# Feed-forward of a two-block transformer kernel: one 512-column operand against the high weights, 256 columns against the low weights

## What is computed

```python
x = x + 0.5 * swiglu(rms_norm(x, gain), w_gate, w_up, w_down)

def rms_norm(x, g):
    y = x * lax.rsqrt(jnp.mean(x * x, axis=-1, keepdims=True) + 1e-6)
    return y * g

def swiglu(x, w_gate, w_up, w_down):
    return (jax.nn.silu(x @ w_gate) * (x @ w_up)) @ w_down
```

## Time and profile before

| what | value |
|---|---|
| time, median of 3 runs | 1128.37 us (1127.51 to 1128.53) |
| profiled execution | 1127.42 us, of which the span is 1125.6 us |
| granted TensorE clock over the span | 0.994 of 2.4 GHz |
| TensorE busy (matmul) | 1109.3 us, 99%, 8842 matmuls |
| VectorE, ScalarE, GpSimd busy | 62%, 51%, 13% |
| DMA | 200.2 MB, 178 GB/s on average |

### The profile page before, as it was taken

How to read it: one execution, slowest core, us unless ns; L and a number is a source line. 1 busy time by engine, 2 the same in 40 slices (tenths; PEclk the granted TensorE clock), 3 DMA queues, 4 the chain that set the end, 5 groups by cost and what they waited for, 6 DMA issues and landing times.

```text
span 1125.6 us, 22927 instructions
## 1 busy us (share of the span) xinstructions
PE 1109.3 (99%) x8842; PEld 1086.3 (97%) x8842; DVE 697.3 (62%) x953; ACT 571.3 (51%) x826; POOL 145.9 (13%) x181
## 2 busy tenths in 40 slices
PE   8999999998999999999999999999999999999997
PEld 7999999887999999999999999999999999999997
DVE  6655655687786555557565555677856667666543
ACT  6544444564664444445444444544655555444541
POOL 3311100025031111011111100000200012111100
PEclk9999999998999999999999999999999999999998
DMA  8755555553356555556556555545565546555551
GB/s 283 262 185 178 178 188 187 168 165 99 95 174 200 185 176 180 187 169 190 186 185 186 177 182 166 188 168 187 183 189 175 183 148 208 187 185 186 178 179 38
DMA packets 55581, 200.20 MB, mean 178 GB/s; under 512 B 6304, under 2 KB 6304, under 8 KB 55392
## 3 DMA queue, kind: packets, MB, share of 16 engines
q1 hardware_dynamic: 54576, 196.11, 54.1%
q0 software_dynamic: 512, 2.65, 0.6%
q10 hardware_dynamic: 432, 0.57, 0.2%
HBM read 198.26 MB, written 1.05 MB: 177 GB/s over the span
## 4 chain that ended last, share of the span: by engine, by line
PE 93%; DVE 3%; POOL 1%; ACT 1%; DMA 1%; issue 0%; ACTq 0%; DVEq 0%; POOLq 0%
PE pair L1131 30%; PE pair L1132 30%; PE pair L1133 30%; DVE x_hl L744 1%; DVE w_lo L738 1%; PE pair L1345 1%; DMA x<-x_in 1%; POOL x_sq L378 1%; POOL x_sq L370 1%; PE pair L1355 0%; DVE x L755 0%; PE pair L1411 0%; PE pair L1454 0%; POOL qk_a L361 0%; PE pair L1366 0%
## 5 line engine op out<-in xcount | busy, mean ns | idle before, releaser
L738 DVE TENSOR_TENSOR w_lo<-w_raw,w_hi 128x1024 fp32r<-128x1024 f32 x369 | 457.3, 1246 | 347.8 <-ACT w_hi L425 346.6
L1131 PE MATMUL pair<-x_hl,w_hi 128*128 128x256 f32 x1792 | 508.8, 284 | 2.6 <-DVE x_hl L744 1.7
L1132 PE MATMUL pair<-x_hl,w_hi 128*128 128x256 f32 x1792 | 507.1, 283 | 0.0
L1133 PE MATMUL pair<-x_hl,w_lo 128*128 128x256 f32 x1792 | 507.0, 283 | 0.0
L425 ACT ACTIVATE w_hi<-w_raw 128x1024 fp32r<-128x1024 f32 x369 | 386.4, 1054 | 234.1 <-PE pair L1133 221.2
L1131 PEld LDWEIGHTS pair<-x_hl,w_hi 128*128 128x128 f32 x1792 | 343.9, 192 | 4.2 <-issue 2.3
L1132 PEld LDWEIGHTS pair<-x_hl,w_hi 128*128 128x128 f32 x1792 | 343.9, 192 | 0.1
L1133 PEld LDWEIGHTS pair<-x_hl,w_lo 128*128 128x128 f32 x1792 | 343.9, 192 | 0.0
L1131 PE MATMUL pair<-wide,w_hi 128*128 128x256 f32 x960 | 273.3, 285 | 0.7 <-DVE wide L932 0.7
L1132 PE MATMUL pair<-wide,w_hi 128*128 128x256 f32 x960 | 272.3, 284 | 0.0
L1133 PE MATMUL pair<-wide,w_lo 128*128 128x256 f32 x960 | 272.2, 284 | 0.0
(11 more groups left out here) (164 smaller groups left out, 558.4 us busy)
## 6 DMA issues: line engine op xcount, KB each, us to landing
w_raw<-stream SPq DMA_DIRECT2D x369, 512.0 KB, 3.5
const<-const_in POOLq DMA_DIRECT2D x1, 1248.0 KB, 7.9
w_raw<-stream SPq DMA_DIRECT2D x4, 256.0 KB, 5.5
out<-x_sq SPq DMA_DIRECT2D x4, 256.0 KB, 2.9
rows<-rows_in POOLq DMA_DIRECT2D x1, 576.0 KB, 9.9
x<-x_in ACTq DMA_DIRECT2D x2, 256.0 KB, 5.5
x<-x_in SPq DMA_DIRECT2D x2, 256.0 KB, 6.6
sgu_w<-sgu_w_in POOLq DMA_DIRECT2D x1, 512.0 KB, 12.9
```

What stands on the lines that cost most here:

```text
L738: nc.vector.tensor_tensor(w_lo[:, slot, :], w_raw[:, slot, :], w_hi[:, slot, :].bitcast(F32), ALU.subtract).then_inc(w_split, 1)
L1131: nc.tensor.matmul(dst, a_hi, b_hi, start=first, stop=False, skip_group_check=True)
L1132: nc.tensor.matmul(dst, a_hi, b_lo, start=False, stop=False, skip_group_check=True)
L1133: return nc.tensor.matmul(dst, a_lo, b_hi, start=False, stop=last, skip_group_check=True)
```

## The change

Three things change, in all four FFNs.

1. TensorE: `three` becomes `both`. The high weights are multiplied with the high and low input in one matmul of 512 columns that fills a bank: columns 0 to 255 get high x high, 256 to 511 high x low. The low weights with the high input, 256 columns, are added to columns 0 to 255.
2. The chain of a chunk: the two halves of a bank have to be added. ScalarE `fetch` copies the second halves of gate and up out of PSUM (128x512) into `low_s`; VectorE `add` adds the first halves (128x512), and then multiplies the gate half alone by `rstd` (128x256). Up is no longer scaled. `hidden` of a chunk moves into the step behind the one that fetches it.
3. Down: `output` sums the two halves of the bank (a reduce over 2 x 256), multiplies by 0.5 and `rstd`, since up wasn't scaled, and adds to x: three instructions in place of one. TensorE reuses a bank when the first of them is done.

```diff
+            def both(dst, a_hi, a_lo, b_hl, first, last):
+
+                nc.tensor.matmul(dst, a_hi, b_hl.rearrange("p a s -> p (a s)"), start=first, stop=False, skip_group_check=True)
+                return nc.tensor.matmul(dst[:, 0:S], a_lo, b_hl[:, 0, :], start=False, stop=last, skip_group_check=True)
...
-                    last = three(dst[:, 0:S], w_hi[:, slot, w], w_lo[:, slot, w], b_hl[:, k, 0, :], b_hl[:, k, 1, :], k == 0, k == KC - 1)
+                    last = both(dst[:], w_hi[:, slot, w], w_lo[:, slot, w], b_hl[:, k, :, :], k == 0, k == KC - 1)
...
ScalarE:
+                def fetch(f, j, i=0):
+                    act.wait_ge(w_used, n0 + 2 * f + 2 + 8 * i)
+                    nc.scalar.activation(low_s[:], pair[j][:, :, S:2 * S], ACT.Copy).then_inc(low_copied, 1)
...
                 def step(f, i=0):
+                    fetch(f - 2, f % 4, i)
+                    hidden(f - 3, i)
                     split(n0 + 2 * f + 2, i, 8)
+                    gate(4 * i + (f - 2))
                     split(n0 + 2 * f + 3, i, 8)
-                    gate(4 * i + (f - 2))
-                    hidden(f - 2, i)
...
VectorE:
-                    dve.wait_ge(w_used, used)
-                    nc.vector.tensor_tensor(sum_s, pair[j][:, :, 0:S], rstd[:].unsqueeze(1).to_broadcast([P, 2, S]),
-                                            ALU.mult).then_inc(both_scaled, 1)
+                    dve.wait_ge(low_copied, FC * e + 1 + f)
+                    nc.vector.tensor_tensor(sum_s, pair[j][:, :, 0:S], low_s[:], ALU.add).then_inc(parts_added, 1)
+                    dve.wait_ge(parts_added, FC * e + 1 + f)
+                    nc.vector.tensor_tensor(gate_s, gate_s, rstd[:], ALU.mult).then_inc(gate_scaled, 1)
...
                 def step(f, i=0):
+                    add(4 * i + (f - 2), f % 4)
                     split(n0 + 2 * f + 2, i, 8)
-                    scale(4 * i + (f - 2), 8 * i + (n0 + 2 * f - 2), f % 4)
+                    product(4 * i + (f - 2), f % 2)
                     split(n0 + 2 * f + 3, i, 8)
-                    product(4 * i + (f - 2), f % 2)
...
-                    nc.vector.scalar_tensor_tensor(x[:, m, :], bank[m % 4][:, 0:S], 0.5, x[:, m, :], ALU.mult,
-                                                   ALU.add).then_inc(x_new, 1)
+                    y_s = y_b[:, m % 2, :]
+                    nc.vector.tensor_reduce(y_s, bank[m % 4].rearrange("p (a s) -> p s a", a=2), AX.X,
+                                            ALU.add).then_inc(down_read, 1)
+                    dve.wait_ge(down_read, KC * e + m + 1)
+                    nc.vector.scalar_tensor_tensor(y_s, y_s, 0.5, rstd[:], ALU.mult, ALU.mult).then_inc(y_scaled, 1)
+                    dve.wait_ge(y_scaled, KC * e + m + 1)
+                    nc.vector.tensor_tensor(x[:, m, :], x[:, m, :], y_s, ALU.add).then_inc(x_new, 1)
...
TensorE (ahead of chunk f, and ahead of output slice m):
-                        pe.wait_ge(both_scaled, FC * e + f - 3)
+                        pe.wait_ge(parts_added, FC * e + f - 3)
...
-                        pe.wait_ge(x_new, X_NEW[p] + m - 3)
+                        pe.wait_ge(down_read, KC * e + m - 3)
```

More of the change, by code:

```diff
@@ L207, in build @@
         r_col_done = sem("r_col_done")
-        both_scaled = sem("both_scaled")
+        low_copied = sem("low_copied")
+        parts_added = sem("parts_added")
+        gate_scaled = sem("gate_scaled")
         silu_done = sem("silu_done")
@@ L486, in step @@
                 def step(f, i=0):
+                    fetch(f - 2, f % 4, i)
+                    hidden(f - 3, i)
                     split(n0 + 2 * f + 2, i, 8)
+                    gate(4 * i + (f - 2))
                     split(n0 + 2 * f + 3, i, 8)
-                    gate(4 * i + (f - 2))
-                    hidden(f - 2, i)
[L493 to L496, removed]
+                fetch(0, 2)
+                split(n0 + 8)
+                gate(0)
+                fetch(1, 3)
+                hidden(0)
+                split(n0 + 9)
+                gate(1)
                 for f in range(4, LEAD):
@@ L501, in ffn @@
                         step(LEAD + j, i)
+                fetch(FC - 2, FC % 4)
+                hidden(FC - 3)
                 split(n0 + UP_B + 2)
                 gate(FC - 2)
+                fetch(FC - 1, (FC + 1) % 4)
                 hidden(FC - 2)
+                gate(FC - 1)
                 split(n0 + UP_B + 3)
-                gate(FC - 1)
                 hidden(FC - 1)
@@ L797, in ffn, with add @@
                 inverse_root(p)
-                def scale(f, used, j, behind=True):
-                    if behind:
+                def add(f, j, reused=True):
+                    if reused:
                         dve.wait_ge(hid_done, FC * e + f)
-                    dve.wait_ge(w_used, used)
-                    nc.vector.tensor_tensor(sum_s, pair[j][:, :, 0:S], rstd[:].unsqueeze(1).to_broadcast([P, 2, S]),
-                                            ALU.mult).then_inc(both_scaled, 1)
+                    dve.wait_ge(low_copied, FC * e + 1 + f)
+                    nc.vector.tensor_tensor(sum_s, pair[j][:, :, 0:S], low_s[:], ALU.add).then_inc(parts_added, 1)
+                    dve.wait_ge(parts_added, FC * e + 1 + f)
+                    nc.vector.tensor_tensor(gate_s, gate_s, rstd[:], ALU.mult).then_inc(gate_scaled, 1)
                 def product(f, slot, reused=True):
@@ L814, in step @@
                 def step(f, i=0):
+                    add(4 * i + (f - 2), f % 4)
                     split(n0 + 2 * f + 2, i, 8)
-                    scale(4 * i + (f - 2), 8 * i + (n0 + 2 * f - 2), f % 4)
+                    product(4 * i + (f - 2), f % 2)
                     split(n0 + 2 * f + 3, i, 8)
-                    product(4 * i + (f - 2), f % 2)
[L821 to L824, removed]
+                add(0, 2, e > 0)
+                split(n0 + 8)
+                product(0, 0, e > 0)
+                add(1, 3)
+                split(n0 + 9)
+                product(1, 1, e > 0)
                 for f in range(4, LEAD):
@@ L829, in ffn @@
                         step(LEAD + j, i)
+                add(FC - 2, FC % 4)
                 split(n0 + UP_B + 2)
-                scale(FC - 2, n0 + UP_B - 2, FC % 4)
                 product(FC - 2, FC % 2)
-                scale(FC - 1, n0 + UP_B, (FC + 1) % 4)
+                add(FC - 1, (FC + 1) % 4)
+                product(FC - 1, (FC + 1) % 2)
                 split(n0 + UP_B + 3)
-                product(FC - 1, (FC + 1) % 2)
                 def output(m):
@@ L1216, in ffn @@
                         slot = (n0 + c) % RING
-                        last = three(bank[4 + c][:, 0:S], w_hi[:, slot, w], w_lo[:, slot, w], x_hi[:, k, :], x_lo[:, k, :], k == 0, k == KC - 1)
+                        last = both(bank[4 + c][:, :], w_hi[:, slot, w], w_lo[:, slot, w], x_hl[:, k, :, :], k == 0, k == KC - 1)
                         if k == KC - 1:
@@ L1253, in ffn @@
                             pe.wait_ge(hid_split, FC * e + k + 1)
-                        last = three(bank[m % 4][:, 0:S], w_hi[:, n % RING, w], w_lo[:, n % RING, w], hid_hi[:, k, :],
-                                     hid_lo[:, k, :], k == 0, k == FC - 1)
+                        last = both(bank[m % 4][:, :], w_hi[:, n % RING, w], w_lo[:, n % RING, w], hid_hl[:, k, :, :], k == 0,
+                                    k == FC - 1)
                         if tile % KC == KC - 1:
```

12 lines of the change are left out of this document (8 added, 4 removed).

## The result

| | before | changed |
|---|---|---|
| median of the runs, us | 1127.94 (4) | 1100.53 (4) |
| lowest to highest, us | 1126.2 to 1128.53 | 1099.32 to 1105.03 |
| profiled execution: time, span, us | 1127.42, 1125.6 | 1099.32, 1097.5 |

The ratio is 0.9767, 95% interval 0.9736 to 0.9797: 27 us faster, as forecast (1101). What the forecast didn't have is the spread: the kernel before holds its times within 0.2%, the changed one doesn't. Some 2 us of spread both have, and they go with the granted TensorE clock over the span: of the executions of the kernel before that ran beside the experiments, those at 0.995 took 1125.9 to 1126.9 us, those at 0.992 took 1128.2 to 1128.7. The rest is the changed kernel's own, and experiment 11 shows what it is.

The account below looks back on a forecast made before the run. TensorE's own pace was taken to bound the kernel: 1127.4 - 27.7 + 0.3 + 0.2 = 1100.2 us for the profiled execution, median 0.95 above, so 1101 us. Own range 1095 to 1107 (71%); 8 in 10 between 1090 and 1112.

Parts of the forecast that it names:

- The pace of the pair: TensorE in the FFNs: 512 + 256 columns take 346.6 ns, saving 13.4 ns through a fixed 13.3 ns per matmul.
- The 5 us that the prediction works out from the Trainium skill: TensorE: by the page's 2.5 ns between matmuls, the pair would save only that a triple, 5 us in all.
- The first rival: TensorE: alternation keeps the slow 512s, the pair takes 351 ns, gain 19 to 8 us, 1109 to 1120; 13%.
- the prediction's own sign (wrong with 351): FFN trace: 0.347 us a pair; right if the sum is within 3 ns, wrong with 351 or 340.
- How many: Four FFNs: 2112 triples, 48 gain nothing at starts, so 2064 x 13.4 ns = 27.7 us saved.
- The chain: Chunk work: VectorE 4.03 us, ScalarE 3.52, under TensorE's 5.55; cost nothing, cover 1.4 us a chunk.
- The 4.1 us that I followed step by step: ScalarE and VectorE, one step with hand-overs, without TensorE's waits: the loop closes in about 4.1 us.
- The fourth rival: ScalarE-VectorE handshake becomes the bound: a round of 6.0 us, not 4.1, makes TensorE wait in gate and up, 1140; 4%.
- The start of an FFN: VectorE's splits of blocks 8 to 10, second FFN: slack 2.3, 1.7, 1.2 us; cost nothing, at worst 1 us each FFN.
- Output and the seam: Down's output slice takes 1.6 us, reduce 0.69; second-to-third FFN seam: low part ready 4.8 us after start, cost 0.3 us.
- The end: Program's end: last square ends at 1115.5, before the last sums at 1116.3; hidden with 0.8 us to spare.
- The sum: Whole kernel: 1127.4 - 27.7 + 0.3 + 0.2 for a start or two = 1100.2 us for the profiled execution.

Follow-up runs that it names:

- experiment 11: The changed kernel again, unaltered, in the same rounds as another variant, for its spread: 1102.92 us (6 runs, 1099.82 to 1111.93).
- experiment 1: The changed kernel with its matmuls cut back to three of 256 columns, other engines as changed: 1127.36 us, ratio to before 0.9998.
- experiment 2: The kernel before with only the matmuls changed to 512 + 256 columns, high x low left out of the FFNs' sums: 1102.03 us, ratio 0.9769.
- experiment 6: The changed kernel with N needless 128x256 multiplications more on VectorE in every chunk: 1103.98 us with N = 2, 1118.9 with N = 5.
- experiment 5: The changed kernel with a chunk's chain not spread over two steps, both splits first on ScalarE and VectorE: 1140.72 us, ratio to before 1.0121.
- experiment 9: The changed kernel with pairs also in the second mixer's gates loop and one plain fp32 matmul ahead of that loop: 1098.8 us, ratio to before 0.9741.
- experiment 10: The changed kernel with pairs also in the second mixer's gates loop and the low-weight matmul first in each pair: 1097.89 us, ratio to before 0.9745.
- experiment 3: The changed kernel with the low-weight product as two matmuls of 128 columns, one more load a triple: 1328.61 us (one run).

## Why the prediction was right, point by point

- **The pace of the pair** was right and right for its reason: 346.5 against 346.6. The fixed 13.3 ns is per matmul in the sum, and alternation adds nothing to it at the lower level. Experiments 1 and 2 give the whole gain to this term. The 5 us that the prediction works out from the Trainium skill (TensorE: Matmul & The Clock Gate, "Back-to-back issue gap") didn't come: the section gives its N/2.4 + 2.5 ns for an isolated matmul, without a weight load's share, and here every matmul loads weights.
- **The first rival** (slow 512s stay, 351 and more) is right in part: at the upper level the pair takes 353. I saw its sign in the earlier trace rows, 0.231 against 0.2266, and read it as a matter of a few steps behind other work. It lasts a whole FFN, in some executions. By the prediction's own sign (wrong with 351) the pace in those FFNs is wrong. The execution with three of them took 1111.93, in that rival's 1109 to 1120 and outside my range of 1095 to 1107. That the forecast hit the median of the result to 1 us owes something to luck: by the times only one of its four runs had an FFN at the upper level, and the six runs of experiment 11 have a median of 1102.92.
- **How many** was right: 27.7 us forecast, 28.1 between the profiled executions. About 1 us of the 28.1 is the clock's, 0.994 before and 0.995 after, by the times of the kernel before at each of the two.
- **The chain** cost 0, as put. Its terms: fetch 0.58 (0.59), add 0.685 (0.685), multiplication 0.461 (0.425), product 0.424 (0.426). The multiplication was a little short, by the work beside it (below). The cover was 1.4 by my sum, which added durations that overlap, and at least 1.7 by experiment 6.
- **Why it costs 0** is its order. The working of the loop by engine sums alone would have passed experiment 5 too, and that one loses 40 us. The 4.1 us that I followed step by step was the argument that counted. The fourth rival, which named this danger, had its price too low: it counted the rounds and not the wait at the start of the down part.
- **The start of an FFN.** VectorE's splits of blocks 8, 9 and 10 in the second FFN, with the start of block 4, answering to the earlier trace rows:

```profile
311.67 0.58 PE L1162 MATMUL pair<-x_hl,w_hi 128*128 128x512 f32 x1
...
318.74 1.22 DVE L755 TENSOR_TENSOR w_lo<-w_raw,w_hi 128x1024 fp32r<-128x1024 f32 x1
...
321.77 1.21 DVE L755 TENSOR_TENSOR w_lo<-w_raw,w_hi 128x1024 fp32r<-128x1024 f32 x1
...
324.79 1.21 DVE L755 TENSOR_TENSOR w_lo<-w_raw,w_hi 128x1024 fp32r<-128x1024 f32 x1
```

  They end at 319.96, 322.98 and 326.0; at 2.77 a block they are wanted at 322.75, 325.5 and 328.3. Slack 2.8, 2.5, 2.3, where I had 2.3, 1.7, 1.2: no cost. From one block to the next the splits come 3.0 apart, where I had 3.4 and 3.2.
- **Output and the seam.** The reduce took 0.684 (0.69). The third FFN starts at 483.81 and the last low part of its input is ready at 487.91 + 0.48, 4.6 us later, before the 4.85 at which it is wanted (I had 4.8):

```profile
483.81 0.39 PE L1162 MATMUL pair<-x_hl,w_hi 128*128 128x512 f32 x1
...
487.91 0.48 DVE L761 SCALAR_TENSOR_TENSOR x_hl<-x,cols,x_hl 128x256 fp32r<-128x256 f32 x1 [0.58 <-ACT x_hl L438]
```

  TensorE doesn't wait; my 0.3 us was 0. In its place the wait for `x_hl` at the program's start grew from 1.7 to 2.6 us: a faster TensorE waits longer for the input.
- **The end** is hidden, as put. The last square is done at 1087.65; the sums' last four matmuls, of 32 over 3.63 us from 1085.39, start near 1088.4, 0.8 later:

```profile
1087.23 0.42 ACT L434 ACTIVATE x_sq<-x 128x256 f32<-128x256 f32 x1 [5.90 <-DVE x L869]
...
1085.39 3.63 PE L1484 MATMUL pair<-ones,x_sq 128*128 128x1 f32 x32
```

- **The sum**, 1100.2 for the profiled execution, came to 1099.32. The 0.2 for the starts shows in the wait for `w_lo`, 0.8 before and 1.0 now; the seam's 0.3 wasn't lost, about 1 us is the clock's (above), and the rest is under what can be told. I named too few things that could make the time spread: the terms were all of one execution.

## What to carry to other kernels

Where matmuls stand close behind each other and a fixed cost per matmul can be read off two lengths, put operands side by side so that one load serves more columns, and pay for it with adds on engines that idle: here 13.4 ns x 2064. Before that is counted as free, follow one round of the hand-overs between the engines, not their sums: the same instructions in another order made the kernel 1.2% slower instead of 2.3% faster. And compare such a kernel by several runs, with counts over equal stretches of each.

## What the runs showed of the hardware that was not expected

- **Two levels of an alternating pair.** 346.5 or 353 ns at a granted clock of 1.00, held for 60 us and more and different between FFNs of one execution and between executions of one program. Three 256s have no such levels: the kernel before and experiment 1 stay within 0.2%, and that much goes with the clock. Where the traces show it change, the even stream is broken. In the profiled execution of the changed kernel blocks 2 and 3 of the second FFN run at the upper level, 14 pairs in 4.94 us, 353 ns; behind the matmul of the squares the lower one begins, block 5 to block 6 in 2.77 us, 346 ns. In experiment 6 with N = 5 it goes up within the second FFN's down part, at 439.0, where a single step from a 512 to its 256 takes 0.34 us. The first and the last 512 of those 14 pairs, and a count behind 439.0:

```profile
306.13 0.39 PE L1162 MATMUL pair<-x_hl,w_hi 128*128 128x512 f32 x1
...
311.07 0.40 PE L1162 MATMUL pair<-x_hl,w_hi 128*128 128x512 f32 x1
```

```profile
440.00:500.00 60.00, 60.00 (x341) 52.05 (x341) 39.63 (x53) 27.67 (x37) 5.18 (x7) 1.00 0.59 189
```

  What picks the level is open. An fp32 matmul ahead isn't enough (experiment 9), and it isn't the chain (experiment 2). With the low product first, no run of ten is above 1101.2, and the two profiles have all FFNs at the lower level; with the high product first, profiles of experiments 2, 6, 9 and 11 have FFNs at the upper, and five of the ten runs of the changed kernel are 3 us or more above its fastest run at the same clock. That suggests that the order helps; the gates loop of experiment 10 stands at the upper level in spite of it, so it isn't the rule.
- **One more load of 128x128 fp32r weights**, for the same columns in two halves of 128, costs 0.11 us (experiment 3).
- **The clock can fall behind a short wait.** TensorE stood for 2.9 us in experiment 5 and 2.1 us in experiment 6, after long work at 2.4 GHz, and then got 1.2 GHz for 3.4 us, 1.7 us of work lost besides the wait. It isn't always so: one of the four waits of 2.9 us in experiment 5 has the clock at 1.00 behind it.
- **GpSimd and VectorE slow each other.** GpSimd's low part of `hid` took 753 ns in the kernel before and 984 in the changed one, whose order puts it beside VectorE's splits. First the kernel before, then three rows of the changed one:

```profile
L330 POOL TENSOR_TENSOR wide<-hid_b,wide 128x256 fp32r<-128x256 f32 x88 | 66.2, 753 | 417.0 <-ACT wide L483 417.0
```

```profile
320.83 0.74 POOL L336 TENSOR_TENSOR wide<-hid_b,wide 128x256 fp32r<-128x256 f32 x1 [11.26 <-ACT wide L493]
...
321.06 0.79 DVE L823 TENSOR_TENSOR tmp<-tmp,rstd 128x256 f32<-128x256 f32 x1
...
336.18 0.99 POOL L336 TENSOR_TENSOR wide<-hid_b,wide 128x256 fp32r<-128x256 f32 x1 [4.32 <-ACT wide L493]
```

  Of the 88, the 76 that begin inside a split of VectorE take 1022 on average, the 10 that begin beside the addition L821, which has one input in PSUM, take 743. Who starts second pays: at 321.06 VectorE's multiplication begins while GpSimd works, and takes 0.79 in place of 0.43; at 336.18 GpSimd begins inside a split of VectorE (335.34, 1.23) and takes 0.99 in place of 0.74. The Trainium skill (SBUF — State Buffer, "SBUF: two separate sides") says that the two engines hold a shared port pair in turn, the whole instruction long, where VectorE has two inputs in SBUF; these rows agree in kind: inside the addition with one input in PSUM nothing is lost. It costs this kernel nothing: TensorE never waits for it.
